# Top-256 selection before sparse attention: a bitwise search for each row's 256th score in place of 32 rounds of maxima

## What is computed

```python
def block(args):                                    # one block of 128 tokens
    qb, iqb, iwb, start = args
    tpos = start + jnp.arange(Q_BLOCK)
    sc = jax.nn.relu(jnp.einsum('bthd,bsd->bths', iqb, ik))
    score = jnp.einsum('bth,bths->bts', iwb, sc).astype(jnp.float32)
    admissible = key_chunk[None, :] <= (tpos // CHUNK)[:, None]
    score = jnp.where(admissible[None], score, -jnp.inf)
    vals, sel = lax.top_k(score, topk)              # topk = 256
    valid = jnp.isfinite(vals)
    ...                                             # attention over the selected keys
```

## Time and profile before

| what | value |
|---|---|
| runs, us | 3084.45, 3085.62, 3090.66 |
| median of the runs | 3085.62 us |
| span of the profiled execution (first to last instruction) | 3082.7 us |
| median less span | 2.9 us |
| PE busy | 2716.7 us (88%) |
| VectorE busy | 1667.3 us (54%) |
| ScalarE busy | 1010.7 us (33%) |
| POOL busy | 877.4 us (28%) |
| MAX8, 192 instructions | 160.8 us |
| MATCH_REPLACE8, 192 instructions | 166.5 us |
| mean granted TensorE clock | 0.941 |

### The profile page before, as it was taken

The page is one execution under the profiler, slowest core; times in us unless marked ns, Lnnn a source line. Parts: engine busy times, 40 slices in busy tenths (PEclk is TensorE's granted clock), DMA queues, the critical chain, the costliest instruction groups (busy, mean ns, idle before and its releaser), DMA issues.

```text
span 3082.7 us, 38906 instructions
## 1 busy us (share of the span) xinstructions
PE 2716.7 (88%) x12584; PEld 2190.4 (71%) x12584; DVE 1667.3 (54%) x3179; ACT 1010.7 (33%) x1882; POOL 877.4 (28%) x423
## 2 busy tenths in 40 slices
PE   7899996778799699999999969566696999999997
PEld 5598774555578588888888857344485888888886
DVE  4699997667745733333433451566646343333346
ACT  5525334556611522221111251444414112222112
POOL 2013874222312322222222221333323212222222
PEclk9999998999999799999999989677797999999999
DMA  4543433111234311111111225322253111111113
GB/s 132 75 90 96 103 103 127 45 45 41 66 144 167 134 48 41 54 48 48 50 51 48 84 88 146 87 57 58 70 176 116 48 41 54 41 54 48 48 47 109
DMA packets 226619, 241.11 MB, mean 78 GB/s; under 512 B 10242, under 2 KB 192546, under 8 KB 222164
## 3 DMA queue, kind: packets, MB, share of 16 engines
q1 hardware_dynamic: 217028, 222.44, 25.3%
q10 hardware_dynamic: 9216, 16.78, 1.9%
q0 software_dynamic: 272, 0.62, 0.1%
HBM read 173.21 MB, written 66.58 MB: 78 GB/s over the span
## 4 chain that ended last, share of the span: by engine, by line
PE 57%; DVE 8%; issue 5%; ACT 4%; ACTq 0%; POOL 0%; DMA 0%; DVEq 0%; SPq 0%; POOLq 0%
PE ps L350 55%; ACT logits L1018 2%; PE ps L1653 1%; DVE row_min_all L1383 1%; PE ps L1623 1%; DVE prob_sums L1393 1%; ACT probs_T L1032 1%; DVE acc L1140 1%; DVE acc L1452 1%; DVE logits L1370 1%; DVE probs_T L1412 1%; ACT junk L791 1%; DVE newton L1110 1%; DVE xn_T L1203 1%; DVE newton L1111 0%
## 5 line engine op out<-in xcount | busy, mean ns | idle before, releaser
L350 PE MATMUL ps<-xn_T,w_split 128*128 128x512 f32 x4608 | 1059.6, 392 | 8.5 <-DVE xn_T L1203 8.5
L350 PEld LDWEIGHTS ps<-xn_T,w_split 128*128 128x128 f32 x4608 | 869.1, 189 | 193.2 <-DVE xn_T L1203 9.4
L350 PE MATMUL ps<-w_split,hidden 128*128 128x512 f32 x4224 | 962.5, 389 | 4.0 <-DVE acc L1452 2.1
L350 PEld LDWEIGHTS ps<-w_split,hidden 128*128 128x128 f32 x4224 | 792.2, 188 | 172.0 <-DVE acc L1452 3.8
L307 POOL TENSOR_TENSOR w_split<-w_raw,w_split 128x1024 fp32r<-128x1024 f32 x192 | 459.1, 2401 | 1587.1 <-ACT w_split L300 1587.0
L1452 DVE TENSOR_TENSOR acc<-acc,ps 128x512 f32<-128x512 f32 x672 | 459.8, 687 | 402.5 <-PE ps L350 402.3
L300 ACT ACTIVATE w_split<-w_raw 128x1024 fp32r<-128x1024 f32 x192 | 197.4, 1049 | 776.7 <-PE ps L350 769.7
L1467 DVE TENSOR_TENSOR sq_h<-relu_h 128x512 f32<-128x512 f32 x128 | 88.6, 693 | 544.3 <-ACT relu_h L1080 544.3
L350 PE MATMUL ps<-probs_T,v_split 128*64 128x512 f32 x612 | 211.5, 459 | 53.2 <-DVE probs_T L1412 52.1
L1080 ACT ACTIVATE relu_h<-ps 128x512 f32<-128x512 f32 x128 | 76.8, 600 | 484.9 <-PE ps L350 484.9
L350 PE MATMUL ps<-k_split,q_tile 128*128 128x256 f32 (+3 forms) x640 | 177.5, 382 | 62.7 <-DVE row_min L1370 43.4
(11 more groups left out here) (157 smaller groups left out, 2067.4 us busy)
## 6 DMA issues: line engine op xcount, KB each, us to landing
w_raw<-in_w SPq DMA_DIRECT2D x128, 512.0 KB, 3.9
hidden<-cat_scratch SPq DMA_DIRECT2D x12, 2048.0 KB, 7.8
q_scratch<-q_split SPq DMA_DIRECT2D x128, 128.0 KB, 2.4
q_tile<-q_scratch ACTq DMA_DIRECT2D x64, 256.0 KB, 2.6
cat_scratch<-attn_out_split SPq DMA_DIRECT2D x128, 128.0 KB, 2.4
w_raw<-in_w_in SPq DMA_DIRECT2D x30, 512.0 KB, 4.4
h_scratch<-acc SPq DMA_DIRECT2D x24, 512.0 KB, 4.1
h_in<-h_scratch SPq DMA_DIRECT2D x24, 512.0 KB, 4.2
```

Of the source, the lines that this page charges most:

```text
L350: return nc.tensor.matmul(out_ap, stat, mov, start=start, stop=stop)
```

## The change

The 256th score of each row is found as a bit pattern. `cand` starts at zero (read as float32 it is the bound); from bit 31 down to bit 0 a bit is tried and kept if at least 256 scores of the row are not below the bound. Rows are held in two groups of three blocks, `picks` = (7, 4, 3) and (6, 5, 2). For each bit and group there are three counts (`count`: a tensor_scalar over the whole row that compares with the bound, writes a byte flag nobody reads, and hands over the sum), one `refuse` (128x3, plain tensor_scalar: was the count below 256, times the bit) and one `move` (128x3, two tensors and an immediate, exclusive or on int32). The refusal and the move of one group stand between the counts of the other. The normalizer stands behind the counts of bit 6. At the end `select` runs per block: a counting pass for what lies strictly above the bound, a compare for equality, a scan that numbers the ties behind that count, two scalar_tensor_tensor that combine rank and comparison, and a multiplication by MASKED.

`flag`, `rank` and `tie` lie at 62 KB to 74 KB of the region in which k2st, vhl, v_ln_split (`vln`) and the bias lines have their places too. So VectorE waits, before the first write, for `line_sp` and `kv_sp` (both spills landed), and ScalarE waits for all eight masks before its first v_ln_split.

```diff
-    m8 = const("max8", [P, 2, 8])
+    cand = const("sel_bound", [P, 2, 3], I32)
+    step_r = const("sel_step", [P, 2, 3], I32)
+    cnt_ge = const("sel_count", [P, 2, 3])
+    cnt_gt = const("sel_above", [P, 2, 3])
...
+    flag = at("sel_flag", [P, 2, 3, 1024], U8, D0 + 62 * K)
+    tie = at("sel_tie", [P, 1024], F32, D0 + 70 * K)
+    rank = at("sel_rank", [P, 1024], F32, D0 + 66 * K)
...
             if g:
                 act.wait_ge(b_full, B_SV + 2 * g)
+            else:
+                act.wait_ge(mask_ok, 8)
             nc.scalar.activation(vln[:, 0], gv[:, :, g * P:(g + 1) * P], ACT.Copy).then_inc(vl_hi, 1)
...
-        def topk(pair):
-            rows = [masks[:, mask_off(b):mask_off(b) + (b + 1) * P] for b in pair]
-            base = tkc[0]
-            with dve.Fori(0, TOPK // 8 // 4, 1) as i:
-                for r in range(4):
-                    c = base + 4 * r + 16 * i
-                    for e in range(2):
-                        dve.wait_ge(tk, c + e + 1)
-                        own_wait(dve)
-                        nc.vector.max(m8[:, e], rows[e]).then_inc(tk, 1)
-                    for e in range(2):
-                        dve.wait_ge(tk, c + e + 3)
-                        own_wait(dve)
-                        nc.vector.match_replace(rows[e], m8[:, e], rows[e], NEG_SEL).then_inc(tk, 1)
-            tkc[0] += TOPK // 2
-            for e in range(2):
-                dve.wait_ge(tk, 2 + tkc[0])
-                nc.vector.tensor_scalar(rows[e], rows[e], -2.0e38, MASKED, ALU.is_ge, ALU.mult).then_inc(mask_ok, 1)
-
-        dve.sem_inc(tk, 2)
-        topk((7, 2))
-        dve.wait_ge(ln_sq, 1)
-        rstd(rsv, sdv, sqv)
-        nc.vector.tensor_tensor(nmr[:], negmu[:], rsv[:], ALU.mult).then_inc(ln_nm, 1)
-        topk((6, 3))
-        topk((5, 4))
+        picks = [(7, 4, 3), (6, 5, 2)]
...
+        def count(e, k, ready):
+            b = picks[e][k]
+            dve.wait_ge(tk, ready)
+            return tick(nc.vector.tensor_scalar(flag[:, e, k, 0:(b + 1) * P], row(b), cand[:, e, k:k + 1].bitcast(F32), None,
+                                                ALU.is_ge, ALU.add, accum_out=cnt_ge[:, e, k:k + 1]))
+
+        def refuse(e, bit, counted):
+            dve.wait_ge(tk, counted)
+            return tick(nc.vector.tensor_scalar(step_r[:, e], cnt_ge[:, e], float(TOPK), -1.0 if bit == 31 else float(1 << bit),
+                                                ALU.is_lt, ALU.mult))
+
+        def move(e, bit, refused):
+            dve.wait_ge(tk, refused)
+            if bit:
+                return tick(nc.vector.scalar_tensor_tensor(cand[:, e], cand[:, e], 1 << (bit - 1), step_r[:, e],
+                                                           ALU.bitwise_xor, ALU.bitwise_xor))
+            return tick(nc.vector.tensor_tensor(cand[:, e], cand[:, e], step_r[:, e], ALU.bitwise_xor))
...
+        def select(e, k):
+            b = picks[e][k]
+            w = (b + 1) * P
+            bound = cand[:, e, k:k + 1].bitcast(F32)
+            tick(nc.vector.tensor_scalar(flag[:, 0, 0, 0:w], row(b), bound, None, ALU.is_gt, ALU.add, accum_out=cnt_gt[:, e, k:k + 1]))
+            n = tick(nc.vector.tensor_scalar(tie[:, 0:w], row(b), bound, None, ALU.is_equal))
+            dve.wait_ge(tk, n)
+            n = tick(nc.vector.tensor_tensor_scan(rank[:, 0:w], tie[:, 0:w], tie[:, 0:w], cnt_gt[:, e, k:k + 1], ALU.add, ALU.bypass))
+            dve.wait_ge(tk, n)
+            n = tick(nc.vector.scalar_tensor_tensor(tie[:, 0:w], rank[:, 0:w], float(TOPK), tie[:, 0:w], ALU.is_gt, ALU.mult))
+            dve.wait_ge(tk, n)
+            n = tick(nc.vector.scalar_tensor_tensor(row(b), row(b), bound, tie[:, 0:w], ALU.is_lt, ALU.add))
+            dve.wait_ge(tk, n)
+            nc.vector.tensor_scalar(row(b), row(b), MASKED, None, ALU.mult).then_inc(mask_ok, 1)
+
+        dve.wait_ge(line_sp, 32)
+        dve.wait_ge(kv_sp, 32)
+        dve.wait_ge(v_ch, chain[0])
+        start = tick(nc.vector.memset(cand[:], 0))
+        ready = [start, start]
+        counted = [0, 0]
+        for bit in range(31, -1, -1):
+            for e in range(2):
+                o = 1 - e
+                back = bit + 1 - e
+                count(e, 0, ready[e])
+                if back < 32:
+                    refused = refuse(o, back, counted[o])
+                count(e, 1, ready[e])
+                if back < 32:
+                    ready[o] = move(o, back, refused)
+                counted[e] = count(e, 2, ready[e])
+            if bit == 6:
+                normalizer()
+        ready[1] = move(1, 0, refuse(1, 0, counted[1]))
+        dve.wait_ge(tk, ready[1])
+        for e in range(2):
+            for k in range(3):
+                select(e, k)
```

More of the change, by code:

```diff
@@ L20 @@
 F32R = mybir.dt.float32r
+U8 = mybir.dt.uint8
+I32 = mybir.dt.int32
 ALU = mybir.AluOpType
@@ L45 @@
 NEG_OUT = -1.0e38
-NEG_SEL = -3.0e38
 MASKED = 1.0e30
@@ L1265, in dve_program @@
                 link(nc.vector.memset(masks[0:HD, mask_off(b) + w - HD:mask_off(b) + w], NEG_OUT))
-        tkc = [0]
-        def topk(pair):
-            rows = [masks[:, mask_off(b):mask_off(b) + (b + 1) * P] for b in pair]
-            base = tkc[0]
-            with dve.Fori(0, TOPK // 8 // 4, 1) as i:
-                for r in range(4):
-                    c = base + 4 * r + 16 * i
-                    for e in range(2):
-                        dve.wait_ge(tk, c + e + 1)
-                        own_wait(dve)
-                        nc.vector.max(m8[:, e], rows[e]).then_inc(tk, 1)
-                    for e in range(2):
-                        dve.wait_ge(tk, c + e + 3)
-                        own_wait(dve)
-                        nc.vector.match_replace(rows[e], m8[:, e], rows[e], NEG_SEL).then_inc(tk, 1)
-            tkc[0] += TOPK // 2
-            for e in range(2):
-                dve.wait_ge(tk, 2 + tkc[0])
-                nc.vector.tensor_scalar(rows[e], rows[e], -2.0e38, MASKED, ALU.is_ge, ALU.mult).then_inc(mask_ok, 1)
@@ L1288, in dve_program, with tick, row @@
-        dve.sem_inc(tk, 2)
-        topk((7, 2))
-        dve.wait_ge(ln_sq, 1)
-        rstd(rsv, sdv, sqv)
-        nc.vector.tensor_tensor(nmr[:], negmu[:], rsv[:], ALU.mult).then_inc(ln_nm, 1)
-        topk((6, 3))
-        topk((5, 4))
+        picks = [(7, 4, 3), (6, 5, 2)]
+        issued = [0]
+        def tick(ins):
+            ins.then_inc(tk, 1)
+            issued[0] += 1
+            return issued[0]
+        def row(b):
+            return masks[:, mask_off(b):mask_off(b) + (b + 1) * P]
@@ new lines, in move, with normalizer @@
+        def move(e, bit, refused):
[4 more added lines that the diff above has]
+            return tick(nc.vector.tensor_tensor(cand[:, e], cand[:, e], step_r[:, e], ALU.bitwise_xor))
+        def normalizer():
+            dve.wait_ge(ln_sq, 1)
+            rstd(rsv, sdv, sqv)
+            nc.vector.tensor_tensor(nmr[:], negmu[:], rsv[:], ALU.mult).then_inc(ln_nm, 1)
```

## The result

The changed kernel takes **3164.58 us** (median of 4 runs, 3162.56 to 3166.12), the kernel before beside it 3086.33 us: a ratio of 1.0253, 95% interval 1.0239 to 1.0268. It is slower by 78 us; the forecast was 3162. The profiled execution took 3162.56 us, its span is 3160.8 us, and the mean granted clock of PE is 0.929, where it was 0.941.

The account below looks back on a forecast made before the run. Projections on PE set the time, with the selection beside them, so new waits count: masks at 420 us, PE at 430 for 353, 77 us on a 3082.7 us span, plus 2.9 us to the runs' median: 3162 us, range 3105 to 3190.

Parts of the forecast that it names:

- What bounded the kernel before: End of the selection: it ends 3.5 us before anybody needs it, so a quicker selection alone gives nothing.
- Start: First count waits for the spill of the bias lines: 178.2 us, where the old selection began at 158.2.
- One bit: Six counts at 1.055 ns a column plus fixed costs, refusals and moves: 5.38 us; 26 bits are 139.8 us.
- Blocks: Small DVE updates stand while POOL operations run: 23.5 us before the normalizer, 17 us from there to the masks.
- Rival 1: The 128x3 operations escape POOL, so no blocks: 3122 us. Chance 0.12.
- rival 2: A count streams two columns at a time, with POOL's blocks; a bit is 3.17 us: 3100 us. Chance 0.07.
- Normalizer: Ready after 26 of 32 bits at 343 us, 48 us after ACT asks; PE's first delay about 34 us, no addend.
- Finish: After the last bit, per row block counting pass, compare, scan, two two-input passes and multiply: 28.1 us.
- Masks to PE: Masks done at 420 us, PE restarts on gating 9.6 us later at 430 us, for 353: delay 77 us.
- Rigid shift: Everything behind PE's restart on the gating stays ordered as before and moves by 77 us.
- Rival 4: Each new DVE instruction pays 0.1 us more for late waits on DVE's own semaphore, 32 us: 3194 us. Chance 0.08.
- Rival 3: Counts at two columns at a time and no blocks; masks at 315 us, before ACT's gate: 3086 us. Chance 0.07.

Follow-up runs that it names:

- e2: The changed kernel without the wait for the spill of the bias lines before the first count: 3142.2 us, ratio 1.018.
- e3: The changed kernel with scratch tiles in free spots, so ScalarE's first v_ln_split waits for no mask: 3134.46 us, ratio 1.0163.
- e1: The changed kernel with the normalizer moved from behind bit 6 to behind bit 15: 3161.33 us, ratio 1.0250.
- e4: The changed kernel with e2 and e3 together and the normalizer after bit 13, all three waits away: 3092.04 us, ratio 1.0019.
- e8: The kernel before with ten more maxima of 1024 columns on DVE behind its last round: 3096.85 us, ratio 1.0037.
- e7: The changed kernel with counts that write flags but take no sum, decisions left out: 3131.52 us, ratio 1.0143.
- e5: The changed kernel with its small updates (refusal, move) replaced by one-input maxima of eight columns, decisions left out: 3134.05 us, ratio 1.0164.
- e9: e4 plus one refusal and move for all six rows, unread sums on tie comparison and final scaling, earlier a_out_split spill: 3091.0 us, ratio 1.0015.
- e11: e9 with POOL's gain operations of groups 4 to 7 and last gating product and remainder given to DVE: 3086.31 us, ratio 0.9999.

## Why the prediction was right

The time (3162 for 3164.6) and the mechanism held, and the mechanism was shown by taking its parts away: e2 for the start, e3 for the gate, e1 for the normalizer's wait lying inside the gate's, e4 for the three together. That the time came within 3 us is in part luck: the terms were off by up to 6 us each and partly cancelled.

- **What bounded the kernel before:** the prediction gave the selection 3.5 us, up to mask_bias. The first mask_bias does not wait for it; what DVE had free was the 5.10 us up to its own logits (e8). The sum does not use the figure.
- **Start:** forecast 178.2 us, measured 179.14, 20.20 us of it idle on the spill.
- **One bit:** forecast 5.38 us, measured 5.48 where POOL is silent (331.58 to 337.06 us). The slope was 1.044 ns for 1.055; the fixed part of a count was 0.13 us where 0.10 was allowed, (5.48 - 4.41 - 4 x 0.075) / 6. e7 shows that the sum is what holds the count at this slope. That agrees with the Trainium skill, "SBUF — State Buffer", section Who interferes with whom: tensor_scalar reaches the two-port modes, but not in the form that writes its accumulator.
- **Blocks:** forecast 23.5 and 17 us. From start and normalizer, 342.8 - 179.1 - 26 x 5.48 - 1.4 leaves 19.8 us before it and 35 - 19.8 = 15 us after, so 6 us less than forecast; the run without them (e5) was 30.5 us shorter. The same section puts such blocks down to a lock on a port pair that DVE and POOL share; the counts and MAX8 that pass unhindered and the 128x3 updates that do not agree with it. Rival 1 fell with this, and its price too was low: e5, which is its condition made real, measured 3134 us, not 3122. e7 gives rival 2's price as 3131 rather than 3100 us, for the longer updates named there.
- **Normalizer:** forecast 343 us with a wait of 48, measured 342.80 with 48.17. The exact hit is luck: blocks (-3.7), bits (+2.6) and start (+0.9) cancel. Forecast PE gap about 34 us, measured 33.92.
- **Finish:** forecast 28.1 us, measured 33.4 (391.4 to 424.8). Mis-sized was the scan, priced at one two-input pass: 1.055 ns a column was taken and 2.08 measured, 4.3 us over 4224 columns. "DVE: opcode table, instruction layouts, handler registers and perf-mode slots", section Datapath and trigger behaviour, in the Trainium skill has it at half throughput, and the trace agrees; taking the page's value would have been better. The other microsecond is in the operations' fixed parts, about 0.19 us each over the 36 where 0.16 was allowed.
- **Masks to PE:** forecast 420, 9.6 and 430 us; measured 424.8, 9.4 and 434.26, a delay of 81.0 for 77. ACT's wait at its gate was 40.80 us for 33 and PE's gap 50.35 for 45. The errors of the blocks (-6), the finish (+5.3, of it the scan 4.3), the bits (+3.2) and the start (+0.9) partly cancel.
- **Rigid shift:** forecast that all later work moves by the delay. It moved by 77.1 us at mask_bias, so 4 us came back in the gating (116.9 us from its first to its last matmul for 121.0), and that return, which was not forecast, hid the scan's error in the total. There DVE, before, had worked beside PE; now it was silent, and PE's granted clock was higher. The same stretch of the gating, 81 us apart, the kernel before and then the one after (PE, PEld, DVE, ACT, POOL, clock, DMA):

```profile
390.00:475.00 85.00, 83.23 (x391) 67.76 (x389) 85.00 (x155) 27.96 (x37) 60.58 (x27) 0.92 0.33 109
```

```profile
471.00:556.00 85.00, 78.23 (x388) 63.52 (x387) 0.00 (x0) 28.98 (x38) 62.92 (x28) 0.97 0.38 127
```

There 388 matmuls took 78.23 us where 391 had taken 83.23. That the silent DVE is the reason for the clock wasn't tested; PE's own 50 us of rest just before the gating is a rival.

- **Rival 4** (0.1 us more for each new instruction) fell: updates that meet nothing take 0.16 us, and their starts cost 0.07. **Rival 3** was never in reach: it needed counts of two columns at a time and no blocks; e7 had the first and 79 us of updates instead.

## What to carry to other kernels

Count the waits a shorter algorithm brings before its instructions: DVE did 80 us less here and the kernel lost 78, because scratch tiles lay where others still had data (the start's wait and the gate's). The by-product that was put far back, the normalizer, cost nothing beside the gate (e1) and set the pace once the gate was gone (e3). A wait that lies inside a later one cannot be priced by taking it away alone; taking away all three shows nearly everything (e4). And beside a busy POOL choose DVE's operations by their kind: here maxima and comparisons that also sum passed; plain tensor_scalar and two-input ones stood still, however small, and on a path with POOL they lengthened POOL's operations too.

## What was not expected of the hardware

- The hold works in both directions. POOL's 1024-column operation, 2.4 us in the kernel before, took up to 4.05 us beside DVE's scan (e4), and its mean stayed near 2.8 us for v_ln_split in e9 and e11. Plain comparisons do it too: w_split's mean was 2.81 us in e7 for 2.40 in the change. The hold is part of what keeps the version without the waits from gaining.
- A sum that nobody reads makes a pass longer alone (1.22 for 0.69 us at 1024 columns) and shorter beside POOL (1.22 for 2.72).
- The read of the accumulator (80 ns, 192 times) held up nothing behind it: it starts 1.20 us after a count of 1024 columns, the update starts with it, and the next count 0.07 us later.
